# Spreading each token tile's epilogue and the next tile's prologue over the expert loop of a SwiGLU phase

## The reference, cut to what matters

```python
def swiglu(x, w_gate, w_up, w_down):
    return (jax.nn.silu(x @ w_gate) * (x @ w_up)) @ w_down
# layer 0: ff = swiglu(x, ...)                       (1024 -> 3584 -> 1024)
# layer 1: top_val, top_idx = lax.top_k(x @ w_router + b_router, 2)
#          combine = sum(one_hot(top_idx) * softmax(top_val))
#          ff = sum over e of combine[e] * swiglu(x, w_gate[e], w_up[e], w_down[e])
x = layer_norm(DN_ALPHA * x + ff, ln_ffn_g[i], ln_ffn_b[i])
x = x + jax.nn.sigmoid(x @ ple_w_gate[i]) * (p[i] @ ple_w_proj[i])
```

## Time and profile before

| what | value |
|---|---|
| median of 6 runs | 22171.63 us |
| profiled execution, its span | 22086.95 us, 22085.8 us |
| PE busy over the span | 16336.0 us (74%) |
| DVE, ACT, POOL busy | 8725.6, 4161.8, 2658.2 us |
| chain that ended last | PE 68%, DVE 10%, DMA 9%, issue 6%, ACT 4% |
| F0, about 5090 to 7560 us | PE busy 1744.72 of 2470 us, clock 0.72, DMA share 0.54 |
| F1, from about 10860 us to the end | PE busy 9894.62 of 11225 us, clock 0.96, DMA share 0.86 |
| spans, cores 0 to 3 and 4 to 7 (median) | 22069.1 us at clock 0.829, 21809.6 us at 0.844 |

### The profile page before, as it was taken

How to read it: one execution, slowest core, us unless ns; L and a number is a source line. 1 busy time by engine, 2 the same in 40 slices (tenths; PEclk the granted TensorE clock), 3 DMA queues, 4 the chain that set the end, 5 groups by cost and what they waited for, 6 DMA issues and landing times.

```text
span 22085.8 us, 236281 instructions; the slowest of 8 cores (21731.0 to 22085.8 us)
## 1 busy us (share of the span) xinstructions
PE 16336.0 (74%) x74112; PEld 8736.8 (40%) x75136; DVE 8725.6 (40%) x15937; ACT 4161.8 (19%) x8448; POOL 2658.2 (12%) x3688
## 2 busy tenths in 40 slices
PE   4555555555776656655699797997979979899798
PEld 3444344442232244444344343443434434344343
DVE  2444344442222233223244353543435434444344
ACT  2333333331111122222211111111111111111111
POOL 0111111111111111111111111111111111111111
PEclk7767676767777666666799998998989989999899
DMA  1100111015556400000299797997979979889797
GB/s 24 16 10 14 16 16 16 8 16 85 89 88 104 78 11 9 12 12 11 42 142 143 115 143 114 143 143 115 142 115 142 143 114 143 125 133 143 114 143 119
DMA packets 1624900, 1827.65 MB, mean 83 GB/s; under 512 B 206856, under 2 KB 1329160, under 8 KB 1623568
## 3 DMA queue, kind: packets, MB, share of 16 engines
q0 software_dynamic: 1484864, 1668.43, 50.7%
q1 hardware_dynamic: 138832, 144.04, 2.1%
HBM read 3413.51 MB, written 67.11 MB: 158 GB/s over the span
## 4 chain that ended last, share of the span: by engine, by line
PE 68%; DVE 10%; DMA 9%; issue 6%; ACT 4%; POOL 2%; DVEq 0%; SPq 0%; ACTq 0%; POOLq 0%
PE ps L174 67%; DVE t L202 5%; DVE t L225 4%; ACT t L196 3%; POOL t L202 2%; DMA t<-x1s 2%; DMA t<-ple_w_gate 1%; DMA t<-ab_w_out 1%; DMA t<-x3s 1%; DMA t<-x2s 1%; DVE t L218 1%; ACT L196 1%; PE ps L178 1%; ACT t L229 1%; DVEq L107 0%
## 5 line engine op out<-in xcount | busy, mean ns | idle before, releaser
L174 PE MATMUL ps<-t 128*128 128x512 bf16 (+6 forms) x68224 | 14577.9, 375 | 3391.5 <-DVE t L202 991.2
L174 PEld LDWEIGHTS ps<-t 128*128 128x128 bf16 (+4 forms) x69248 | 7486.7, 121 | 10484.0 <-issue 5021.2
L202 DVE TENSOR_TENSOR t<-ps,t 128x512 f32<-128x512 f32 (+3 forms) x5256 | 3095.7, 601 | 2140.3 <-PE ps L174 1491.4
L202 DVE TENSOR_TENSOR t<-t,ps 128x512 f32<-128x512 f32 (+1 forms) x2144 | 1474.8, 688 | 5926.1 <-PE ps L174 5734.4
L196 ACT ACTIVATE t<-ps 128x512 f32<-128x512 f32 (+3 forms) x2544 | 1435.5, 564 | 9897.4 <-PE ps L174 9884.6
L174 PE MATMUL ps<-t,cst_sb 128*128 128x256 f32 (+3 forms) x3584 | 1392.0, 546 | 1568.1 <-ACT t L196 1429.5
L202 DVE TENSOR_TENSOR t<-t 128x512 bf16<-128x512 f32 (+6 forms) x3264 | 1858.9, 580 | 1044.0 <-ACT t L196 741.7
L196 ACT ACTIVATE t<-t 128x256 f32<-128x256 f32 (+6 forms) x2945 | 1248.0, 450 | 3731.4 <-DVE t L225 1514.1
L174 PEld LDWEIGHTS ps<-t,cst_sb 128*128 128x128 f32 (+1 forms) x3584 | 876.8, 264 | 2031.3 <-issue 1905.8
L202 POOL TENSOR_TENSOR t<-t 128x256 f32<-128x256 f32 (+3 forms) x1152 | 966.9, 861 | 5154.1 <-DVE t L202 3234.2
L225 DVE SCALAR_TENSOR_TENSOR t<-t 128x256 f32<-128x256 f32 (+2 forms) x2648 | 1280.4, 484 | 410.1 <-ACT t L196 165.2
(11 more groups left out here) (33 smaller groups left out, 1412.0 us busy)
## 6 DMA issues: line engine op xcount, KB each, us to landing
t<-moe_w_gate POOLq DMA_DIRECT2D x448, 1024.0 KB, 10.8
t<-moe_w_up POOLq DMA_DIRECT2D x448, 1024.0 KB, 16.3
t<-moe_w_down POOLq DMA_DIRECT2D x448, 1024.0 KB, 13.6
t<-ffn_w_gate POOLq DMA_DIRECT2D x56, 1024.0 KB, 8.4
t<-ffn_w_up POOLq DMA_DIRECT2D x56, 1024.0 KB, 11.9
t<-ffn_w_down POOLq DMA_DIRECT2D x56, 1024.0 KB, 10.6
t<-ab_w_out POOLq DMA_DIRECT2D x128, 256.0 KB, 4.4
t<-ple_w_gate POOLq DMA_DIRECT2D x32, 1024.0 KB, 9.5
```

The source lines that it names most:

```text
L174: return self.op("pe", lambda: self.nc.tensor.matmul(out.ap, lhsT.ap, rhs.ap, start=start, stop=stop, **kw), [out], [lhsT, rhs])
L202: return self.op(eng, lambda: self._ve(eng).tensor_tensor(out.ap, a.ap, b.ap, op), [out], [a, b])
```

## The change

Two generators take over the prologue and the epilogue: `P_gen(t)` and `Q_gen(t)`, cut by `yield` into steps. `experts(t, pumpfn)` runs the blocks of tile t and calls `pumpfn` after each. `pumpfn` emits the next steps of a chain made of Q of the tile before and then P of the tile after: one step after each block in F1, six in F0. P of the first tile stands ahead of everything, Q of the last behind everything. `xf`, `xb`, `y` and `combT` get two copies; the epilogue reuses `xb` for its bf16 input, gets scratch tiles of its own (`tmpq`) and one buffer of its own for `ple_w_gate` (`wpgb`). What is computed, and each step's instructions, stay the same.

```diff
-    for t in range(NTW):
-        t0 = t * TW
+    def P_gen(t):
+        par = t % 2; t0 = t * TW
         for c in range(8):
-            fw.dma("sp", xf("a", A, c, F), xin((t, c), sl(c * 128, 128), sl(t0, TW)))
-        fw.copy(xb("a"), xf("a"), eng="act")
+            fw.dma("sp", xf[par]("a", A, c, F), xin((t, c), sl(c * 128, 128), sl(t0, TW)))
+        yield
+        fw.copy(xb[par]("a"), xf[par]("a"), eng="act")
+        yield
...
+    def Q_gen(t):
+        par = t % 2; t0 = t * TW
+        yv = y[par]; xx = xf[par]; xxb = xb[par]
+        ln_feature_major(cx, ph, [yv("a", A, c, F) for c in range(8)], 8,
...
+        yield
+        fw.copy(xxb("a"), xx("a"), eng="act")
+        yield
+        load_x_tile_T(cx, di["p"].h[layer], t0, TW, None, pTb, xin_rot, nchunks=2)
+        yield
+        for half in range(2):
+            fw.dma("pool", wpgb("a"), View(di["ple_w_gate"].h[layer][:, half * 512:(half + 1) * 512].rearrange("(k p) c -> p k c", p=128), []))
+            yield
+            for d4 in range(4):
...
+                fw.act(sg("a"), pg("a", A, F), AF.Sigmoid)
+                fw.tt(sg("a"), sg("a"), pp("a", A, F), ALU.mult)
...
+                    fw.tt(yv("a", A, dc, F), sg("a"), xx("a", A, dc, F), ALU.add, eng="pool")
+                yield
...
+    for _ in P_gen(0):
+        pass
+    prevQ = None
+    kstep = 1 if moe else 6
+    for t in range(NTW):
+        gens = []
+        if prevQ is not None:
+            gens.append(prevQ)
+        if t + 1 < NTW:
+            gens.append(P_gen(t + 1))
+        chain = itertools.chain(*gens)
+
+        def pumpfn():
+            for _ in range(kstep):
+                next(chain, None)
+        experts(t, pumpfn)
+        for _ in chain:
+            pass
+        prevQ = Q_gen(t)
+    for _ in prevQ:
+        pass
```

More of the change, by code:

```diff
@@ L984, in phaseC @@
     cx.ps = Rot(cx.psb[0:6])
+import itertools
 def phaseF(cx, layer, xin, xout_scratch):
@@ L1010, in phaseF @@
         fw.dma("sp", sel8("a"), di["sel8"]("a"))
-        combT = ph.sb([8, TW])
+        combT = [ph.sb([8, TW]) for _ in range(2)]
         combB = ph.sb([128, TW])
         rt = ph.rot(2, [128, 176])
-    xf = ph.sb([128, 8, TW]); xb = ph.sb([128, 8, TW], BF16); xxb = ph.sb([128, 8, TW], BF16)
-    y = ph.sb([128, 8, TW])
+    xf = [ph.sb([128, 8, TW]) for _ in range(2)]
+    xb = [ph.sb([128, 8, TW], BF16) for _ in range(2)]
+    y = [ph.sb([128, 8, TW]) for _ in range(2)]
     wgb = ph.rot(2, [128, 8, 512], BF16); wub = ph.rot(2, [128, 8, 512], BF16); wdb = ph.rot(2, [128, 4, 1024], BF16)
+    wpgb = ph.sb([128, 8, 512], BF16)
     hb = ph.rot(8, [128, TW], BF16)
     tmpr = ph.rot(4, [128, TW])
+    tmpq = ph.rot(4, [128, TW])
     stat = [ph.sb([128, TW]) for _ in range(4)]
@@ L1034, in phaseF @@
                 for kc in range(8):
-                    fw.mm(ps("a", A, sl(g * 8, 8)), xf("a", A, kc, gs), Wr("a", A, kc, slice(0, 8)), start=(kc == 0), stop=(kc == 7))
+                    fw.mm(ps("a", A, sl(g * 8, 8)), xf[par]("a", A, kc, gs), Wr("a", A, kc, slice(0, 8)), start=(kc == 0), stop=(kc == 7))
             r = rt.get()
@@ L1059, in phaseF @@
                 fw.mm(ps2("a", slice(0, 8), sl(g * 128, 128)), r("a", A, sl(128 + g * 8, 8)), cx.ident)
-            fw.copy(combT("a"), ps2("a", slice(0, 8), F), eng="act")
+            fw.copy(combT[par]("a"), ps2("a", slice(0, 8), F), eng="act")
+            yield
+    def Q_gen(t):
+        par = t % 2; t0 = t * TW
+        yv = y[par]; xx = xf[par]; xxb = xb[par]
+        ln_feature_major(cx, ph, [yv("a", A, c, F) for c in range(8)], 8,
+                         [lng("a", A, slice(c, c + 1)) for c in range(8)], [lnb("a", A, slice(c, c + 1)) for c in range(8)],
+                         [xx("a", A, c, F) for c in range(8)], sq_rot=tmpq, stat=stat, TW=TW)
+        yield
+        fw.copy(xxb("a"), xx("a"), eng="act")
+        yield
+        load_x_tile_T(cx, di["p"].h[layer], t0, TW, None, pTb, xin_rot, nchunks=2)
+        yield
+        for half in range(2):
+            fw.dma("pool", wpgb("a"), View(di["ple_w_gate"].h[layer][:, half * 512:(half + 1) * 512].rearrange("(k p) c -> p k c", p=128), []))
+            yield
+            for d4 in range(4):
+                dc = half * 4 + d4
+                pg = cx.ps.get(); pp = cx.ps.get()
+                for kc in range(8):
+                    fw.mm(pg("a", A, F), wpgb("a", A, kc, sl(d4 * 128, 128)), xxb("a", A, kc, F), start=(kc == 0), stop=(kc == 7))
+                for kc in range(2):
+                    fw.mm(pp("a", A, F), Wpp("w", A, kc, sl(dc * 128, 128)), pTb("a", A, kc, F), start=(kc == 0), stop=(kc == 1))
+                sg = tmpq.get()
+                fw.act(sg("a"), pg("a", A, F), AF.Sigmoid)
+                fw.tt(sg("a"), sg("a"), pp("a", A, F), ALU.mult)
+                if xout_scratch is not None:
+                    o = oT.get()
+                    fw.tt(o("a"), sg("a"), xx("a", A, dc, F), ALU.add, eng="pool")
+                    fw.dma("sp", xout_scratch((t, dc), sl(dc * 128, 128), sl(t0, TW)), o("a"))
+                else:
+                    fw.tt(yv("a", A, dc, F), sg("a"), xx("a", A, dc, F), ALU.add, eng="pool")
+                yield
+        if xout_scratch is None:
+            for g in range(4):
+                ot = otok.get()
+                for d0 in (0, 4):
+                    ps = cx.ps.get()
+                    for d4 in range(4):
+                        fw.transpose(ps("a", A, sl(d4 * 128, 128)), yv("a", A, d0 + d4, sl(g * 128, 128)), cx.ident)
+                    fw.copy(ot("a", A, sl(d0 * 128, 512)), ps("a"), eng="act")
+                fw.dma("sp", cx.out((t, g), sl(t0 + g * 128, 128), slice(0, 1024)), ot("a"))
+                yield
@@ L1061, in phaseF, with experts @@
+    def experts(t, pumpfn):
+        par = t % 2
         for e in range(NE):
@@ L1063, in phaseF @@
                 ps = cx.ps.get()
-                fw.mm(ps("a", A, F), sel8("a", slice(0, 8), sl(e * 128, 128)), combT("a"))
+                fw.mm(ps("a", A, F), sel8("a", slice(0, 8), sl(e * 128, 128)), combT[par]("a"))
                 fw.copy(combB("a"), ps("a", A, F), eng="act")
@@ L1074, in phaseF @@
                     for kc in range(8):
-                        fw.mm(pg("a", A, F), wg("a", A, kc, sl(fc * 128, 128)), xb("a", A, kc, F), start=(kc == 0), stop=(kc == 7))
+                        fw.mm(pg("a", A, F), wg("a", A, kc, sl(fc * 128, 128)), xb[par]("a", A, kc, F), start=(kc == 0), stop=(kc == 7))
                     for kc in range(8):
-                        fw.mm(pu("a", A, F), wu("a", A, kc, sl(fc * 128, 128)), xb("a", A, kc, F), start=(kc == 0), stop=(kc == 7))
+                        fw.mm(pu("a", A, F), wu("a", A, kc, sl(fc * 128, 128)), xb[par]("a", A, kc, F), start=(kc == 0), stop=(kc == 7))
                     sg = tmpr.get()
@@ L1091, in phaseF @@
                     if e == 0 and f == 0:
-                        fw.stt(y("a", A, dc, F), xf("a", A, dc, F), ALPHA, pd("a", A, F), ALU.mult, ALU.add)
+                        fw.stt(y[par]("a", A, dc, F), xf[par]("a", A, dc, F), ALPHA, pd("a", A, F), ALU.mult, ALU.add)
                     else:
[L1094 to L1127, removed]
+                        fw.tt(y[par]("a", A, dc, F), pd("a", A, F), y[par]("a", A, dc, F), ALU.add)
@@ new lines, in experts @@
+                pumpfn()
+    for _ in P_gen(0):
[16 more added lines that the diff above has]
+        prevQ = Q_gen(t)
```

## The result

The changed kernel is slower. Its median is 22898.3 us (10 runs, 22564.85 to 23075.6) beside 22171.98 us for the kernel before on the same chip (20 runs, 21852.15 to 22440.62). That is 726 us more; the forecast was 22990. The ratio of those runs in which no group of cores fell behind at a lower granted clock is 1.028, with a 95% interval from 1.014 to 1.041: it excludes no change, but not a change under 2%. The profiled execution took 22605.96 us (span 22604.8).

A forecast was written before the change was run, and what follows sets the result against it. PE was taken to work nearly without a break inside F1's experts and mostly to wait between tiles. F1's 615 and F0's 201 us summed to 816 more, which added to 22171.63 gave 22990 us; range 22500 to 23450.

The forecast's parts named there:

- 63 and 21 held blocks: Blocks over 7 tiles whose weights are issued late: nine per tile in F1, three per tile in F0.
- One d4 in F1: Block behind one embedding-gate step d4 in F1 ends at T+43.3 instead of T+22.0: 21.3 us more, eight times 170.4.
- The price of the low clock: Ten matmuls of a held block run at the low clock after PE's idle time: 2.2 us per block.
- LayerNorm in F1: Block behind LayerNorm in F1 ends at T+67.4, 45.4 us above the pitch.
- The pair's price from a free queue: Time from the issue of `wg` to the landing of `wu`, issued into a free queue: 14.0 us.
- The rest of a tile in F1: p, router, combine and output transposes, 27.3 us, plus the wait for p, 1.8: 29.1 us per F1 tile.
- F0: forecast 201: Three held blocks per F0 tile cost 67.0, 44.2 and 51.3, 162.5 in place of 133.8: 28.7 more, 7 times 201 us.
- F1 in sum: An F1 tile pays 244.9 in place of 157.0 us: 87.9 more, 7 times 615.
- (a): Rival: weights come in time and PE's idle time between tiles goes; 1301 us less, 20870; chance 0.06.
- (b): Rival: held blocks take F1's loaded landing, `wu` 18.0 us after `wg`; 252 us more, 23242; chance 0.16.
- (c): Rival: the clock limit of 0.81 reaches F1 as well; 2195 us more, 25185; chance 0.03.
- (d): Rival: losses and gains cancel, low bounds hold and F0 wins its tile ends; 21660 or up to 22507; chance 0.06.

The follow-up runs named there:

- e3: Kernel before plus one POOL addition behind each of the first eight blocks of an F1 tile, reading that block's sum; 24088.35 us beside 23304.43.
- e1: Changed kernel with the additions of step d4 on DVE instead of POOL; 23270.5 us beside 23304.43 for the kernel before.
- e2: Changed kernel with the next block's weights issued ahead of the inserted step, arithmetic still on POOL; 22508.65 us beside 23304.43 for the kernel before.
- e7: e2 plus more blocks between x load and cast, and in F0 two early-issued gate-weight buffers and steps spread wider; 22591.56 us beside 23458.79 for before.
- e5: Kernel before, unchanged, profiled once more on the second chip of the experiments; 23458.79 us.
- e8: Control to e3: kernel before with the same added POOL additions, but reading only x, not the block's sum; 23484.7 us beside 23458.79.

## Why the prediction was right

**The mechanism.** The step on which all hung, that an addition in POOL's row turns a weight issue from a block ahead of need to after it, held in every sign named: 63 and 21 held blocks, the issue right behind the addition, no gap where a tile begins, PE waiting 11 to 14 us for `moe_w_gate` behind the first d4 steps, ACT behind the third held block of F0. e3 shows the mechanism in the kernel before, alone; e1 and e2 take it out of the changed kernel in two ways. Two statements beside it were not right. ACT does have more to do, the 140 table loads; e2 has as many, and its blocks with a step d4 take no longer for them. And the two copies of `wg` were not free since the experts ended, because `ple_w_gate` uses them until the embedding gate's last matmul; only the other copies were. Neither is a term of the sum.

**One d4 in F1: forecast 21.3, measured 20.4 on average.** T is 12235.9 in the tile shown. PE starts the step without the 1.0 of idle time; the addition starts at T+4.8 (forecast 5.5), `wg` goes out at T+6.0 (6.8), and `wu` lands 13.5 after that (14.0). Where the clock came back at once, the block stands 39.86 behind the last one (12229.47 to 12269.33), which is 17.9 over 21.97. The price of the low clock, put at 2.2 for each block, was paid only in some. Over the 288 such blocks of six cores, all without 0.81, the price went from 17.8 to 25.9.

**LayerNorm in F1: forecast 45.4, measured 47.8 in the tile shown.** POOL was through at T+29.7 (30.95 forecast); then six issues went out at once, since the block behind the next one could be loaded too, and `wu` landed 17.5 after `wg`, not 14.0. The pair's price from a free queue didn't fit a burst.

**The rest of a tile in F1: 29.1 was called an upper value, and two of its terms were too small.** The cast of the next x, taken as covered, cost 9.0, and the wait for p 5.0 in place of 1.8. In the tile of 1488.0 us on core 5 the eight d4 cost 161.0 (forecast 170.4), LayerNorm 47.3 (45.4) and so the rest 37.9 (29.1). The tile as a whole comes out, 1488.0 - 1241.8 = 246.2 against 244.9, because the cheaper d4 pay for the dearer rest; that much of the agreement is luck.

**F0: forecast 201, measured 147.** Two things make up the 54, about half each. The cast of the next x was counted behind the third held block of seven tiles and comes in six: the last tile has no next one, its third block cost 25.6 instead of 51.3, and the tile as a whole lost nothing. And the six other tiles lost some 24 each, not 28.7 (core 4: 301 to 308 us in place of 278 to 283). Their first held blocks cost 62 to 64 (forecast 67.0), the second 40 to 44 (44.2), the third 49 to 53 (51.3). These were priced at the 0.81 of core 0 and ran without it. The step failed in its count, not in its mechanism.

**F1 in sum: forecast 615, measured 650 on core 4.** Of this 43 belong to one tile of 1532 us (core 4), a fifth of whose time ran at 0.81; without it 607.

**The sum: forecast 816, 768 on average over cores 4 to 7, 726 by the medians.** On core 4 (841) F0 came 54 short and F1 35 over, and 44.5 more stand ahead of F0 and between the two phases, where the change has nothing; on cores 6 and 7 these parts were 22 and 46 shorter after than before, so they scatter. The slowest core lost only 519 from one profiled execution to the other, because core 0, the slowest before, ran F0 at 0.81, with 312 to 316 us per tile and not 280, while in the changed kernel's no core had 0.81 in F0. The forecast was made against that execution and took the clock to be the same after. How the other runs behind the two medians spent their clock in F0 is not on record, so the 92 us by which the forecast is too high cannot be divided up. That the sum came this close is in part luck.

**The rivals.** (a) fell with the first held block, and e2 and e7 show what it would have taken. (b), a landing of 18.0 in F1's own traffic, is refuted for d4 (13.5; the median over all loads of `moe_w_up` fell from 16.3 to 14.1), and came close for LayerNorm's burst (17.5). (c), 0.81 in F1, was seen on other chips, with the kernel before as well (e5), and nothing here shows that the change brings it on. (d) fell with (a).

## What to carry to other kernels

An engine that issues DMAs in its row prefetches only as far as its row lets it: before work is interleaved into a loop, look at what that engine does in the inserted steps, and put the next loads' issues ahead of any instruction that waits for the loop's own results. Two copies of a buffer don't help if the issue stands behind such a wait, while the same arithmetic, on the same engine, costs nothing once its inputs are there (e8) or the issue is past it (e2). And a count of steps per tile is to be made for the first and the last tile apart.

## What was not expected of the hardware

**0.81 by pairs of cores.** The granted clock of 0.81 (between the two levels of 1.2 and 2.4 GHz) did not always come by dies. In the kernel before it held cores 0 to 3 in F0 and none of cores 4 to 7. But in e7 it held cores 0 and 1 in F0 and cores 2 and 3, which belong to the same die, in F1. The stretches of e7, cores 0 and 2, in F0:

```profile
6000.00:6400.00 400.00, 375.17 (x1375) 153.62 (x1374) 121.01 (x173) 88.00 (x115) 73.13 (x70) 0.79 0.75 126
...
6000.00:6400.00 400.00, 343.90 (x1458) 153.32 (x1487) 135.27 (x194) 98.57 (x126) 80.80 (x77) 0.93 0.79 135
```

and the same two cores in F1:

```profile
15000.00:16000.00 1000.00, 951.94 (x4392) 432.23 (x4390) 488.40 (x717) 135.71 (x210) 118.32 (x139) 0.99 0.92 145
...
15000.00:16000.00 1000.00, 957.69 (x3597) 399.59 (x3669) 413.82 (x609) 100.06 (x162) 93.66 (x112) 0.81 0.76 120
```

In the same 1000 us PE is busy for 952 and 958 us on both, and does 4392 matmuls on the one and 3597 on the other. Cores 4 to 7 split in the same way into 4, 5 and 6, 7, and in the profiled execution of the changed kernel all eight cores ran F1 almost wholly without 0.81. The Trainium skill ("TensorE: Matmul & The Clock Gate", Part 1, the note on the peak-current limiter) speaks of a whole die, from its third dense core on and as long as the load lasts; these rows differ in the first point. In the second e5 differs: its core 0 had 0.81 for seven to nine tenths of the time in its first tiles of F1 (1645 us the first), and none of it in the fifth (1404 us), under the same work. What decides which pair is held stays open.

**The wait for x in e3 and e8** is at least 7 us shorter than before, though nothing was done to it. The rows give a likely cause. Before, POOL issues the weights of two blocks, six loads, in one go (12275.51 to 12279.78), and SP's eight loads of x go out beside them over 35.72 us. In e8 (core 6) the first added addition stands between the two blocks' issues: three go out from 13680.21 on, the next three only at 13729.10, when the addition has waited 45.12 us for that x, and the eight loads take 29.20 us. No run tests this by itself.
